# Gated delta net in a two-block layer kernel: the last tile's norm split in two, its Z products and weight panel moved, its last state update left out, the first decay moved up

## The reference

```python
def step(state, inp):
    qd, ke, u_c, w_c, qk_c, gl = inp
    v_new = u_c - jnp.einsum('bhcd,bhde->bhce', w_c, state)
    o = jnp.einsum('bhcd,bhde->bhce', qd, state) + jnp.einsum('bhij,bhje->bhie', qk_c, v_new)
    state = state * gl[..., None, None] + jnp.einsum('bhcd,bhce->bhde', ke, v_new)
    return state, o
...
o = rmsnorm_2(o, out_norm) * jax.nn.silu(z.reshape(B, S, DN_HEADS, DN_HEAD_DIM).astype(f32))
```

## Time and profile before

| | |
|---|---|
| median of 3 runs | 2784.81 us (2783.25 to 2786.75) |
| the profiled execution: time, span | 2782.94 us, 2781.1 us |
| PE, weight loads busy | 94%, 84% of the span |
| POOL, DVE, ACT busy | 48%, 42%, 35% |
| mean granted clock of PE | 0.959 |
| delta net's pieces and norm, to the attention's first product | about 1591 to 1825 us |

### The profile page before, as it was taken

One profiled execution on the slowest core, in us unless ns is written; L12 is line 12 of the kernel. 1 busy time (PEld: TensorE's weight loads), 2 busy tenths in 40 slices (PEclk: granted clock), 3 DMA queues, 4 the chain that ended last, 5 costly groups with the idle time before them and its releaser, 6 DMA issues.

```text
span 2781.1 us, 47625 instructions
## 1 busy us (share of the span) xinstructions
PE 2613.6 (94%) x18775; PEld 2335.9 (84%) x18775; DVE 1163.4 (42%) x2027; ACT 966.4 (35%) x1715; POOL 1325.3 (48%) x790
## 2 busy tenths in 40 slices
PE   8978999999996999999899799799999989999999
PEld 7957999999994999999878688688877777788887
DVE  6864422125686442122667544201466632230210
ACT  4334322223334332222456321332455552321221
POOL 4761666567574276566844310132211145564562
PEclk9988999999997899999999899899999999999999
DMA  5210222322310022232213000131211143223322
GB/s 156 77 46 16 77 90 78 104 79 79 101 62 31 22 86 87 83 102 74 94 61 121 17 2 2 54 98 61 62 43 44 45 144 106 76 91 102 95 91 76
DMA packets 175677, 203.93 MB, mean 73 GB/s; under 512 B 6435, under 2 KB 160646, under 8 KB 175254
## 3 DMA queue, kind: packets, MB, share of 16 engines
q1 hardware_dynamic: 172176, 199.57, 22.1%
q10 hardware_dynamic: 3334, 2.06, 0.3%
HBM read 193.23 MB, written 8.39 MB: 72 GB/s over the span
## 4 chain that ended last, share of the span: by engine, by line
PE 78%; POOL 6%; issue 4%; DVE 4%; ACT 3%; POOLq 2%; DMA 1%; DVEq 1%; SPq 0%; ACTq 0%
PE ps L729 17%; PE ps L730 16%; PE ps L731 16%; PE ps L1595 6%; POOL wlo L2885 4%; PE ps L980 4%; PE ps L1475 3%; POOLq L2930 2%; PE ps L1457 1%; POOL hn_lo L2892 1%; PE ps L1420 1%; POOL conv L2928 1%; PE ps L1445 1%; PE ps L860 1%; PE ps L1203 1%
## 5 line engine op out<-in xcount | busy, mean ns | idle before, releaser
L2885 POOL TENSOR_TENSOR wlo<-wraw,whi 128x1024 fp32r<-128x1024 f32 x364 | 877.8, 2433 | 914.2 <-ACT whi L1679 914.0
L729 PE MATMUL ps<-hn_hi,whi 128*128 128x264 f32 (+1 forms) x2752 | 891.4, 324 | 23.0 <-POOL wlo L2885 10.2
L730 PE MATMUL ps<-hn_lo,whi 128*128 128x264 f32 (+1 forms) x2752 | 878.8, 319 | 0.0
L731 PE MATMUL ps<-hn_hi,wlo 128*128 128x264 f32 (+1 forms) x2752 | 877.0, 319 | 0.0
L729 PEld LDWEIGHTS ps<-hn_hi,whi 128*128 128x128 f32 x2752 | 522.7, 190 | 62.0 <-issue 16.6
L731 PEld LDWEIGHTS ps<-hn_hi,wlo 128*128 128x128 f32 x2752 | 522.4, 190 | 36.0
L730 PEld LDWEIGHTS ps<-hn_lo,whi 128*128 128x128 f32 x2752 | 523.4, 190 | 31.9
L1679 ACT CAST whi<-wraw 128x2048 fp32r<-128x2048 f32 x182 | 346.5, 1904 | 547.3 <-PE ps L731 369.7
L729 PE MATMUL ps<-ff_hi,whi 128*128 128x264 f32 x704 | 201.1, 286 | 4.1 <-POOL wlo L2885 4.1
L731 PE MATMUL ps<-ff_hi,wlo 128*128 128x264 f32 x704 | 200.4, 285 | 0.0
L730 PE MATMUL ps<-ff_lo,whi 128*128 128x264 f32 x704 | 200.0, 284 | 0.0
(11 more groups left out here) (479 smaller groups left out, 4338.2 us busy)
## 6 DMA issues: line engine op xcount, KB each, us to landing
wraw<-in_w_in SPq DMA_DIRECT2D x54, 1024.0 KB, 5.2
wraw<-in_w_gate_up SPq DMA_DIRECT2D x44, 1024.0 KB, 5.1
wraw<-in_w_up SPq DMA_DIRECT2D x16, 1024.0 KB, 5.4
wraw<-in_w_down SPq DMA_DIRECT2D x16, 1024.0 KB, 5.0
wraw<-in_w_out SPq DMA_DIRECT2D x12, 1024.0 KB, 5.1
wraw<-in_w_down SPq DMA_DIRECT2D x16, 768.0 KB, 4.4
wraw<-in_w_down SPq DMA_DIRECT2D x16, 640.0 KB, 4.0
gate_dram<-gate_out SPq DMA_DIRECT2D x16, 256.0 KB, 2.0
```

Source lines behind the costliest of these rows:

```text
L729: nc.tensor.matmul(dst, whi[:, slot, c:c + P], rhs_hi, start=start, stop=False)
L730: nc.tensor.matmul(dst, whi[:, slot, c:c + P], rhs_lo, start=False, stop=False)
L731: return nc.tensor.matmul(dst, wlo[:, slot, c:c + P], rhs_hi, start=False, stop=stop)
L2885: last = nc.gpsimd.tensor_tensor(wlo[:, slot, part], wraw[:, slot, part], whi[:, slot, part].bitcast(F32), ALU.subtract)
```

## The change

It has five parts.

1. **The norm in two steps.** Tile 2 is squared after piece 12. Variances, root and multiplications of tiles 0 to 2 run during tile 3. Of tile 3, the first chunk is squared after piece 14, the second, a group of heads at a time, after pieces 14 and 15 are added; its variances, root and one multiplication end the norm.
2. **Z products behind the values.** In the last tile the order on PE is now: values 14, Z1, values 15, output 14, Z2, output 15, Z3. Then come T0, T1, Z4, T2, Z5, T3, Z6, T4, Z7, T5, T6, T7.
3. **No last state update.** Pieces 14 and 15 make only the output part.
4. **The third Z panel early.** Tile 3 uses `dw_last` and `dvn_last`, which lie over the keys of `qkv`, so slot 0 is free after piece 11 (`oa_done` 12). ACT rounds the panel after piece 14. The fourth still waits for the end of the squares, now `sq_o_ready` 2.
5. **The first decay first.** `decay_exp(0)` stands ahead of the last three heads of `token_rows`.

```diff
+        dw_last = put("dw_last", [P, DN_HEADS, 2, CHUNK], work + 16384)
+        dvn_last = put("dvn_last", [P, DN_HEADS, P], work + 16384 + 4096)
...
+        def dw_of(t):
+            return dw_last if t == NT2 - 1 else dw_t
...
                 if j == 2:
-                    sp.wait_ge(sq_o_ready, 1)
+                    sp.wait_ge(oa_done, 12)
+                if j == 3:
+                    sp.wait_ge(sq_o_ready, 2)
                 panel(N0 + PN_Z + j, j % 2, w_in_2[:, :, C_Z + PW * j:C_Z + PW * (j + 1)])
...
                 last.then_inc(s_done, 1)
+                out_products(k, t, ch, g)
+
+            def out_products(k, t, ch, g):
+
+                r = half_rows(ch)
+                pe.wait_ge(vn_ready, k + 1)
                 if k:
                     pe.wait_ge(o_added, k)
...
                 state_products(k + 1, t, 0, 1)
-                if more:
-                    level_products(t + 1, 1)
-                else:
+                if not more:
+                    new_values(k + 2, t, 1, 0)
                     z_fill(1)
+                    new_values(k + 3, t, 1, 1)
+                    out_products(k + 2, t, 1, 0)
+                    z_fill(2)
+                    out_products(k + 3, t, 1, 1)
+                    z_fill(3)
+                    continue
...
             for c in range(DN_HEADS):
-                if c >= 4:
-                    z_fill(c)
                 if c == 0:
                     pe.wait_ge(o_normed, NT2)
...
                 last.then_inc(o_turned, 1)
+                if 1 <= c < 5:
+                    z_fill(c + 3)
...
             swish(23)
-            for c in range(21, 24):
-                token_rows(c)
...
+            decay_exp(0)
+            for c in range(21, 24):
+                token_rows(c)
...
+                if k == 12:
+                    tile_squares(NT2 - 2)
+                    act.drain().then_inc(sq_o_ready, 1)
+                if k == 14:
+                    follow(PN_Z, EV_Z + 2)
+                    out_roots(1, 0, NT2 - 1)
+                    out_squares(NT2 - 1, half_rows(0), range(DN_HEADS), 14)
+            out_squares(NT2 - 1, half_rows(1), range(HG), 15)
+            out_squares(NT2 - 1, half_rows(1), range(HG, DN_HEADS), 16)
             act.drain().then_inc(sq_o_ready, 1)
...
+            out_roots(2, NT2 - 1, NT2)
...
-                if c % 2:
+                if c == 1:
+                    follow(PN_Z + 1, EV_Z + 4)
+                if c >= 5 and c % 2:
                     follow(PN_Z + c // 2, EV_Z + c + 1)
...
+                if not more:
+                    next_state(k + 1, t, 0, 1)
+                    nc.vector.tensor_scalar(g_w, sq_q, 1e-6, P * 1e-6, ALU.add, ALU.mult)
+                    dve.drain()
+                    out_variances(1, 0, t)
+                    next_out(k + 2, t, 1, 0)
+                    out_normed(1, 0, t)
+                    next_out(k + 3, t, 1, 1)
+                    out_variances(2, t, NT2)
+                    out_normed(2, t, NT2)
+                    continue
```

More of the change, by code:

```diff
@@ L1236, in new_values @@
                     hh = HG * g + j
-                    last = nc.tensor.matmul(ps[r, 4, tile(j)], dw_t[:, hh, ch, :], state[:, hh, :],
+                    last = nc.tensor.matmul(ps[r, 4, tile(j)], dw_of(t)[:, hh, ch, :], state[:, hh, :],
                                             start=False, stop=True, skip_group_check=True)
@@ L1259, in state_products @@
                     hh = HG * g + j
-                    last = nc.tensor.matmul(ps[r, 7, tile(j)], dqk[t % 2][r, hh, :], dvn[r, hh, :], start=True, stop=True)
+                    last = nc.tensor.matmul(ps[r, 7, tile(j)], dqk[t % 2][r, hh, :], dvn_of(t)[r, hh, :], start=True, stop=True)
                 last.then_inc(oa_done, 1)
@@ L1982, in key_rows @@
                 for ch in range(2):
-                    last = nc.scalar.mul(dw_t[:, :, ch, :], blocks_of(ch, 0, DN_HEADS), -1.0)
+                    last = nc.scalar.mul(dw_of(t)[:, :, ch, :], blocks_of(ch, 0, DN_HEADS), -1.0)
                 last.then_inc(dw_ready, 1)
@@ L1997, in values_out, with out_squares, tile_squares, out_roots @@
                 last.then_inc(oi_ready, 1)
-            def out_squares(t):
-                act.wait_ge(o_added, 4 * t + 4)
-                for hh in range(DN_HEADS):
-                    nc.scalar.activation(junk_o[:, hh % HG, :], k_tok[:, t, hh, :], ACT.Square, accum_out=sq_o[:, t, hh:hh + 1])
+            def out_squares(t, r, heads, added):
+                act.wait_ge(o_added, added)
+                for hh in heads:
+                    nc.scalar.activation(junk_o[r, hh % HG, :], k_tok[r, t, hh, :], ACT.Square,
+                                         accum_out=sq_o[r, t, hh:hh + 1])
                     if hh % HG == HG - 1:
                         act.drain()
-            decay_exp(0)
-            key_rows(0)
+            def tile_squares(t):
+                out_squares(t, slice(0, P), range(DN_HEADS), 4 * t + 4)
+            def out_roots(n, t0, t1):
+                act.wait_ge(o_var, n)
+                nc.scalar.activation(o_inv[:, t0:t1, :], o_inv[:, t0:t1, :], ACT.Sqrt).then_inc(o_rms, 1)
             for k, t, ch, g in pieces():
+                if k == 0:
+                    key_rows(0)
                 values_out(k, t, ch, g)
@@ L2664, in next_state, with out_variances, out_normed @@
                                         ALU.add).then_inc(o_added, 1)
+            def out_variances(n, t0, t1):
+                dve.wait_ge(sq_o_ready, n)
+                nc.vector.scalar_tensor_tensor(o_inv[:, t0:t1, :], sq_o[:, t0:t1, :], 1.0 / P, g_w[:, t0:t1, :],
+                                               ALU.mult, ALU.add).then_inc(o_var, 1)
+            def out_normed(n, t0, t1):
+                dve.wait_ge(o_rms, n)
+                nc.vector.reciprocal(o_inv[:, t0:t1, :], o_inv[:, t0:t1, :])
+                dve.drain()
+                for t in range(t0, t1):
+                    nc.vector.tensor_tensor(k_tok[:, t, :, :], k_tok[:, t, :, :], wide(o_inv[:, t, :], [P, DN_HEADS, P], 2),
+                                            ALU.mult).then_inc(o_normed, 1)
             decay_sums(0)
```

69 lines of the change are left out of this document (24 added, 45 removed).

## The result

Four runs of the changed kernel took 2757.95 us in the median (2754.17 to 2760.11), four of the kernel before 2785.78 (2783.25 to 2788.31): a ratio of 0.9896 (95% interval 0.9879 to 0.9913), 28 us less. The forecast was 2766.0, with a range down to 2761.5, so the direction was right and the gain came out larger than the range allowed. The profiled execution took 2760.11, its span 2758.3, at a mean clock of 0.966 (before 2782.94, 2781.1 and 0.959).

A forecast was written before the change was run, and what follows sets the result against it. PE, busy in 94% of the span, was taken as the bound, with gains only at its waits, low clock or removable work. 18.75 less 1.53 for clock, plus 1.5 for decay, gave 18.7: 2784.81 to 2766.1 us, range 2761.5 to 2772.

The forecast's parts named there:

- step 3: From Z1's end (A) to the attention: Z3 ends at A + 16.37, attention starts 18.75 us earlier at full clock.
- The conditions for PE not to wait: Behind A, other engines finish in time: norm at A + 15.1, 1.3 us spare; fourth panel 4 us spare.
- Step 2: Last tile's state part: two state updates go, saving 2.1 us of PE.
- Step 5: First decay, moved ahead of the last heads of v: gains 1.5 us.
- Rival one: Norm late: POOL slows all three DVE multiplications, T0 waits 1.4 us, time 2767.5; chance 0.09.
- Rival two: Fourth Z panel late: Z6 waits about 1.3 to 6.7 us, time 2767.4 to 2772.8; chance 0.06.
- Rival three: Gain given back behind the delta net, by KC's load or some buffer: 2780 to 2786; chance 0.06.
- Rival four: Low clock from values 14 to T7: L us low lose L/2, all 52 us of work low gives 2817; chance 0.03.
- no drop at 1754: Case inside the forecast: the low clock at 1754 us does not return, time 2764.6.
- term 4: Clock drop at 1754 returns over values 14 and Z1, costing 1.53 us (bounds 0 and 3.1), leaving 17.2.

The follow-up runs named there:

- before, again: The kernel before, unedited, run once more for its own spread: 2784.99 us (10 runs), ratio 0.9993.
- after, again: The changed kernel, unedited, run once more to see what repeats: 2764.73 us (6 runs), ratio 0.9912.
- the version with two KC groups: The changed kernel with the attention's first two KC product groups moved ahead, among the last transposes and silu waits: 2763.3 us (6 runs), ratio 0.9914.
- after, third: The changed kernel, unedited, run a third time in a later set: 2762.27 us (6 runs), ratio 0.9916.

## Why the prediction was right, and where it failed

**What held.** The placing against A (the end of Z1). T0 stood at A + 16.37 in step 3 and came at 1770.68 - 1754.45 = 16.23; the last silu product ended at A + 43.45, forecast A + 43.7. The conditions for PE not to wait held with nearly the margins that were named: the last multiplication ended at 1769.24, 1.4 us ahead of T0 (forecast 1.3); the first multiplication, by the blocking, at A + 7.9 and the third at A + 10.2, both as written. Step 2, the state part, was 2.1 and measured 2.2 when put back. Step 5, the decay, was 1.5 and measured 1.7. One reading in step 3 doesn't follow: 5.96 for a T with a Z, less the 5.70 of a Z, leaves 0.26 for a T, not 0.36. The trace has T0, T1 and Z4 in 6.40 us (1770.68 to 1777.08) and T2 with Z5 in 5.96, so a T is 0.44 and a Z behind it 5.52. These differences nearly cancel in the sum.

**The rivals.** Rival one (norm late): no wait at T0; one multiplication of the three was held up, not all. Rival two: no Z waits for POOL. Rival three: 956.0 to 960.5 us behind the last silu product after, 956.1 and 960.0 before, so nothing is given back that shows. Rival four: 5.6 and 11.9 us busy at the low clock in the tile 3 stretch, against 12.7 and 19.5 before, so the clock was no worse. The case "no drop at 1754", inside the forecast, is what came in all three profiles of the changed kernel; the clock was low only at tile 3's first pieces, as it was before too.

**The step that failed: term 4, the clock**, and with it the range. I took the low clock at 1754 for a property of pieces 12 and 13, and set 1.53 us against the gain for it. It came back in none of the three profiles of the changed kernel, and the repeat of before does not have it either. PE's busy time at the low clock in tile 3's stretch, by its place:

| us | first 16 us | 16 to 30 us | behind | stretch |
|---|---|---|---|---|
| before | 5.6 | 3.4 (at 1754) | 3.8 (behind the norm's wait) | 92.1 |
| after | 5.6 | 0 | 0 | 72.6 |
| before, again | 11.8 | 0 | 7.7 (behind the norm's wait) | 95.4 |
| after, again and third | 11.9 | 0 | 0 | 75.6 |

Rows over the first two of these places in before, and the first three stretches of before again, in the columns of the last row:

```profile
1734.00:1740.00 6.00, 5.57 (x24) 4.84 (x24) 0.00 (x0) 0.92 (x4) 0.87 (x1) 0.50 0.00 0
...
1753.00:1757.00 4.00, 4.00 (x16) 3.18 (x16) 1.73 (x5) 0.00 (x0) 0.00 (x0) 0.62 0.00 0
```

```profile
1719.00:1733.00 14.00, 11.51 (x51) 10.14 (x50) 0.00 (x0) 3.72 (x10) 1.90 (x1) 0.52 0.00 0
1733.00:1772.00 39.00, 37.08 (x208) 29.91 (x207) 6.52 (x20) 6.75 (x30) 0.00 (x0) 1.00 0.00 1
1772.00:1791.00 19.00, 7.29 (x24) 5.68 (x25) 8.91 (x12) 11.32 (x25) 8.10 (x4) 0.56 0.47 146
```

So the first pieces run low for some 7 us or for some 14, in both kernels, and that is the luck of an execution. What stood behind the norm's wait went with the wait. Between profiles with the same first pieces the stretch shrank by 19.5 and by 19.8 us, where term 4 had left 17.2 and the sum without it was 18.75. Of that, 16.0 us are work and waits (15.5 in the sum: 18.75 less 3.3, half of the 6.55 us busy in the two low rows), and 3.6 and 3.8 are the clock, where the sum had it give 3.3 and take 1.5. With the decay's 1.7 the profiles give 21.3 us, between the 18.7 of the sum and the 23.4 ± 3 of all runs. The 2 us that are left I leave unexplained.

The range was too narrow for a simpler reason: its lower bound came from the spread of three runs, 1.56 us below the median. The 55 runs of the same kernel reach from 10.8 below their median to 7.6 above. Nothing in the profile of before told this; the page shows one execution. The first result, 2757.95, was outside the range; 2761.8 over 16 runs is just inside, by 0.3 us, so whether it is met depends on the draw of runs. Leaving term 4 out would not have been enough: without it, and with 1.7 for the decay, the sum gives 2764.4.

**Interaction.** Put back one at a time, the state part costs 2.2 us, the panel 8.0, the norm 4.6 and the order 5.7: 20.5, more than the 16.0 that all together gave. Waits in a row cover each other: before, the norm's wait hid most of the panel's. What each part is worth depends on the others being there. These prices are from one profile each. The medians of the runs are above the 2761.8 of the changed kernel by 4.1 (state), 7.2 (panel), 9.0 (norm) and 0.4 us (order), each uncertain by 4 to 6 us: they bear out the panel and the norm, the state part barely, and the order not.

**What stays open.** Why the first pieces of tile 3 run low for 7 us in one execution and for 14 in the next. (Behind each long wait, the 10.32 us of before and the 7.82, 4.50 and 4.13 us that the experiments put in, the clock was low.) Open too is what brings the drop at 1754. The version with the first decay only and the one with the Z products in the old order, where Z1 follows output 13 as before, both have it. The changed kernel's first profile and the versions with the state kept, the panel late and the norm late, with equally long low first pieces and values 14 behind output 13, do not. But the version with two KC groups has the order of the changed kernel there and has the drop (1752.5 to 1756.5, a clock of 0.61), so the order alone does not decide it.

```profile
1752.50:1756.50 4.00, 4.00 (x26) 3.55 (x26) 2.08 (x7) 0.00 (x0) 0.00 (x0) 0.61 0.02 4
```

## What to carry to other kernels

Before a difference in total time is explained, compare the part that nobody edited between two profiles of the same kernel: here that part alone moved by 20 us, about as much as the whole gain. Measure the change between marks that enclose it, less half of PE's busy time at the low clock in between, and read its parts by putting each back in turn, with the wait that is to reappear predicted first. Expect a wait that is hidden behind another one to show its full length once the first is removed. Give a low clock that one profile shows a range from nothing up, not a fixed price, unless it stands behind a wait that stays.

## What was not expected of the hardware

- The low clock does not always come back at the same place in repeats of one program. Ahead of the last silu the five profiles hold 80.8 us (before, again) to 117.6 us (after, third) of busy time at the low clock. Half the difference between the two of before (115.1 and 80.8) is 17 us, close to the 15 us between their marks. It is not the whole of it: before and the changed kernel's repeat hold 115 us both, and their marks are 5.0 us apart.
- A very small operation is held up as a large one is: DVE's variance step on 128 x 8 elements took 0.17 us in the changed kernel, and 0.62 where POOL's split had been moved beside it (the version with POOL kept off the norm; its timelines of POOL and DVE below). It ended at 1780.64, with POOL's second operation (1780.62). Operations that read PSUM kept their time in the same stretch, 0.69 us for the output's add.

```profile
1775.90 4.72 POOL L2932 TENSOR_TENSOR wlo<-wraw,whi 128x1024 fp32r<-128x1024 f32 x2 [38.95 <-DVE k_tok L2714]
```

```profile
1777.93 0.69 DVE L2699 TENSOR_TENSOR k_tok<-ps,o_scaled 64x512 f32<-64x512 f32 x1 [2.11 <-PE ps L1276]
1780.02 0.62 DVE L2705 SCALAR_TENSOR_TENSOR o_inv<-sq_o,g_w 128x8 f32<-128x8 f32 x1 [1.40 <-ACTq L2049]
```
